# A two-layer encoder step with Strassen products in its channel mixer: loads, copies, additions and splits of the weights put into another order

## The chip, the core and the metric

The kernel runs on one core of one Trainium2 chip, which has a matrix engine (TensorE, PE in the rows), two elementwise engines (VectorE, DVE; ScalarE, ACT), GpSimd (POOL) and SyncE (SP). The metric is the device time in microseconds (us) of one execution. Before the change three runs took 1881.4, 1882.58 and 1882.79 us, so the median is 1882.58 us.

## The reference

Two layers of an encoder, in float32, for a prompt of 528 tokens (16 learned ones and 512) and for 8 running streams of 16 tokens: 656 columns in all, width 1024. Each layer mixes tokens (attention with a latent cache beside a gated recurrence) and then channels. All that the change touches is in the channel mixer:

```python
def conv_ffn(h, p, buf):
    u = h @ p['w_ffn_up']                      # 1024 -> 2 x 2816
    a, v = u[..., :D_FF], u[..., D_FF:]
    ext = jnp.concatenate([buf.astype(a.dtype), a], axis=1)
    c = p['ffn_conv_b'] + sum(ext[:, j:j + T] * w[j] for j in range(3))
    out = (jax.nn.silu(c) * v) @ p['w_ffn_down']   # 2816 -> 1024
    return out, ext[:, -2:]
```

An RMSNorm stands before it and after it, and `x` is added.

## The kernel before, in words

**Layout.** Activations lie with their 1024 features on 128 partitions by 8 tiles, and the 656 tokens along the free dimension, in two halves of 328 (`cols_of(0)`, `cols_of(1)`). Each float32 operand of a product is split into a high part (a copy by ACT into float32r) and a low part (the difference, by DVE), and a product is three matmuls: low weight by high input, high by high, high by low.

**The channel mixer.** The 2816 inner channels are 22 chunks `c` of 128. Chunks 0 to 2 are plain. Chunks 3 to 21 (`NPL` = 3 is the first) are computed with a Strassen scheme, in which the 2x2 blocks are the halves of the 1024 inputs by gate and value weights, and the token halves. A chunk has seven products of 12 matmuls (4 input tiles by 3), in this order: B11, B21, T2, T3, T1, T4, B22. T1 to T4 have sums of weight blocks as weights, and T1 to T3 have sums of input blocks as inputs: `Sf` is such a sum (by DVE, `s_sum`), `Sh` its high and `Sl` its low part (`s_high` by ACT, `s_low` by DVE), slots 0, 1, 2 for T1, T2, T3. T4 and B22 need the second token half of the inputs, of which the lower four tiles of `Hh` and `Hl` are replaced for B22 (`s4_part`).

The chunks form six groups (`GROUPS`): 0-1, 2-5, 6-9, 10-13, 14-17, 18-21. After each group a pass over the down weights (`down_pass`, passes 0 to 5) multiplies its chunks into 8 output tiles `n`. Pass 0 covers the plain chunks 0 and 1 and runs just before chunk 3. In pass 0 ACT copies each tile to `Y`; in later passes DVE adds it to `Y`; in pass 5 DVE and ACT also make the squares for the norm.

**Within a chunk** the PSUM results are taken by `chunk` of ACT (lines 1970 to 1998) and of DVE (2774 to 2802):
- ACT: a convolution step and the `silu` of the chunk before (`pending`), the copy of B11 to `p1` (`act_took` 0), the copy after T2 to `u2` (`act_took` 1), the copy of T3 to `p7` (`act_took` 2), and `g_high` of the chunk before. `p1` and `u2` are halves of `R2` (line 154), whose buffer the rows call R; `p7` is called p.
- DVE: the rest of the convolution (`conv_rest`), two steps that end in `ax`, `times_v` of the chunk before, the low part `g_low` of its result, the addition to `p7` after T1 (`dve_took`), and after T4 the addition to `u2`.
- PE (`chunk`, lines 928 to 975) waits for `act_took` 0 ahead of T2, for `act_took` 1 ahead of T1, for `act_took` 2 ahead of T4, and for `dve_took` ahead of B22. In chunk 3 it also waits for the sums of inputs (`s_split`), which are counted in the order in which DVE makes them.

**Splits of weights.** Weights come in pieces of 512 KB into four raw slots: slots 0 and 1 (`wraw`) and 2 and 3 (`wff`). ACT writes the high part (`w_high`, or `w_high_two` for two half-units that lie side by side), DVE the low part (`w_low`), and DVE's counts `w_split`. A table, `split_after` (lines 502 to 509), says after the end of which PE unit each split may be made; `highs(l, u)` and `lows(l, u)` issue all splits up to unit `u`. With the numbers of this kernel, `highs(l, u0 + B21)` in a later chunk issues the splits of that chunk's own T4 and B22; `highs(l, u0 + T2)` the next chunk's B11 and B21; `highs(l, u0 + T1)` the next T2 and T3; in the pass 0 loop unit `u0` gives chunk 3's T2 and T3, and unit `u0 + 1` its T1 and T4. In chunk 3 `highs(l, u0 + B21)` gives its B22 alone. The last unit of the layer, number `UNITS_L - 1`, is pass 5's last piece and has a buffer of its own (`whi_x`, `wlo_x`).

**What loads.** SP issues the loads of pieces in one fixed order (lines 614 to 654). A load waits until the splits of the piece that was in its slot are done (`earlier`, `last_unit`): the two pieces of chunk c take the slots of chunk c - 2, so that they wait for the splits of that chunk's T4 and B22. SP also loads B22's block into `t2` and `t3`. POOL adds blocks with accumulating DMAs, in one order (lines 781 to 793): for chunk c it issues T1's sum of chunk c + 1 (`sum_t1`, line 736, which waits for that chunk's second piece), then T4's sum of chunk c (`sum_t4`, line 760), then T2's and T3's of chunk c + 1 (lines 744 and 750). In the last chunk of a group T4's sum goes first.

Of the kernel before, what the change touches and what calls it, by code (L numbers as in the profile page):

```python
# [54 lines left out]
P_UP = P_OUT + N_OUT  # L55
# [52 lines left out]
def build(nc, a):  # L108
# [6 lines left out]
    with ctx:  # L115
# [347 lines left out]
        def s_split(l, i):  # L463


            return S_DVE * l + (13, 14, 19, 21)[i]
# [114 lines left out]
        def _(sp):  # L581
# [31 lines left out]

            for g in range(DEPTH * PIECES):
# [29 lines left out]
                if earlier[g] is not None:  # L644
                    sp.wait_ge(S("w_split"), earlier[g] // PIECES * UNITS_L + last_unit(earlier[g] % PIECES) + 1)
                if p == P_CHUNK[NPL]:
                    sp.wait_ge(S("oas_taken"), l + 1)
                    sp.wait_ge(S("ob_split"), HG * (l + 1))
                    sp.wait_ge(S("out"), 32 * (l + 1))
                for s, lo, hi, at in parts_of(p):  # L650
                    sp.dma_start(raw_of(p)[:, at:at + hi - lo], a["wstream"][l, s][:, lo:hi]).then_inc(S(loaded[g][0]), 16)
                for c, p0 in P_CHUNK.items():
                    if p == p0 + 1:
                        sum_parts(l, c)
# [813 lines left out]
        def _(act):  # L1468
# [124 lines left out]
            for l in range(DEPTH):  # L1593
# [376 lines left out]
                def chunk(c, pending):  # L1970
# [10 lines left out]
                    highs(l, u0 - 1)  # L1981
# [6 lines left out]
                    highs(l, u0 + B21)  # L1988
# [11 lines left out]
                for q, (c0, c1) in enumerate(GROUPS):  # L2000
# [11 lines left out]
                    if q == NQ - 1:  # L2012
                        w_high(l, UNITS_L - 1)
                    for n in range(KD):
                        if not q:
                            act.wait_ge(S("down"), down_no(l, q, n))
                            did(f(two(Y[:, n, :]), halves(down_bank(n)), ACT.Copy), "act_took")
                        if not q and n == 5:
                            s_high(Sh[:, 0, :, :], Sf[:, 0, :, :], 18)
                            act.wait_ge(S("tile"), t0 + T_UP + 2 * NPL)  # L2020
                            for x in range(2):
                                s_high(Hh[:, 2 * x:2 * x + 2, cols_of(1)], s4_part(x), 12, -1.0)
                        if q and q < NQ - 1 and nk * (n + 1) % 8 == 0:
                            highs(l, u0 + nk * (n + 1) // 8 - 1)
                        if not q and n >= 5:
                            highs(l, u0 + nk * (n + 1) // 8 - 1)
                exp_table()
                split_to[0] = 0
                for n in range(3):
                    act.wait_ge(S("dve_took"), down_added(l, NQ - 1, n))  # L2030
                    square_x(n0 + N_FFNPOST, n, Y[:, n, :])
                    step(f(Y[:, n, :], Y[:, n, :], ACT.Copy, scale=cols[:, l, C_FFNPOST + n:C_FFNPOST + n + 1]))
                w_high(l + 1, 0)
# [116 lines left out]
        def _(dve):  # L2150
# [173 lines left out]
            for l in range(DEPTH):  # L2324
# [449 lines left out]
                def chunk(c, pending):  # L2774
# [17 lines left out]
                    if pending is not None:  # L2792
                        g_low(pending)
                    after(T1)
                    dve.wait_ge(S("act_took"), act_took(l, c, 2))
                    did(tt_(p7[:, :], p7[:, :], bank(G[s], 0), ALU.add), "dve_took")
                    lows(l, u0 + T1)
# [6 lines left out]
                for q, (c0, c1) in enumerate(GROUPS):  # L2804
# [8 lines left out]
                    else:  # L2813
                        g_low(last_c)
                        lows(l, u0 - 1)
                        for k in range(KH):
                            s_sum(Sf[:, 0, k, :], KH + k, 1, Sf[:, 0, k, :])
                        s_low(2, Sl[:, 0, :, :], Sf[:, 0, :, :], Sh[:, 0, :, :])
                        for x in range(2):
                            s_low(3 + x, Hl[:, 2 * x:2 * x + 2, cols_of(1)], s4_part(x),  # L2820
                                  Hh[:, 2 * x:2 * x + 2, cols_of(1)], -1.0)
# [4 lines left out]
                    if q == NQ - 1:  # L2826
                        w_low(l, UNITS_L - 1)
                    for n in range(KD if q < NQ - 1 else 3):
                        if q:
# [7 lines left out]
                            if q == NQ - 1:  # L2837
                                add_square(n0 + N_FFNPOST, n, n == 0)
                        if q < NQ - 1 and nk * (n + 1) % 8 == 0:
# [220 lines left out]
```

## Time and profile before

| | |
|---|---|
| median of three runs | 1882.58 us |
| the profiled execution | 1880.04 us |
| its span | 1878.2 us |
| granted TensorE clock, mean | 0.992 |
| DVE busy | 1266.8 us, 67% |
| ACT busy | 951.5 us, 51% |
| POOL busy | 230.1 us, 12% |
| HBM read, written | 170.98 MB, 8.65 MB |

The span runs from the first to the last recorded instruction, and 1.84 us of the execution lie outside it. Shares are means over stages with different limits, so the table says who works most and not what a change is worth. The channel mixer's chunks and passes run from about 480 to 925 us in layer 0 and from about 1405 to 1849 us in layer 1.

### The profile page before, as it was taken

Reading aid. Unit: us, or ns where it says so; the run is one execution under the profiler, and the core shown is the slowest. Engines: PE = TensorE matmul, PEld = TensorE weight load, DVE = VectorE, ACT = ScalarE, POOL = GpSimd, SP = SyncE. Lnnn points to the kernel's source line nnn. Section 1 sums busy time; section 2 is a strip of 40 time slices with the busy share of each in tenths; the row PEclk is TensorE's granted clock in tenths of the full one; section 3 lists DMA queues with packets and bytes.
Section 4 is the critical chain, followed back from the end, with each engine's and each line's share of the span. In section 5 each row is a group of like instructions: output and inputs, shape, how many; then the busy total and the mean of one; then the engine's idle time right before and its main releaser. Section 6 shows DMA issues by size and latency. Waiting matters only on the chain.

```text
span 1878.2 us, 31219 instructions
## 1 busy us (share of the span) xinstructions
PE 1803.6 (96%) x11636; PEld 1650.6 (88%) x11636; DVE 1266.8 (67%) x1973; ACT 951.5 (51%) x1593; POOL 230.1 (12%) x257
## 2 busy tenths in 40 slices
PE   8999999999999999999899999999999999999996
PEld 7999976599999999999799999656988999999994
DVE  5777875435775766678767778654377766757777
ACT  6444546435663544535654445564366543635356
POOL 0000023200112121111000000350001121111200
PEclk9999999999999999999999999999999999999998
DMA  5312121411456666655131112314116666666641
GB/s 183 94 58 70 64 74 42 162 45 57 122 140 148 167 152 156 152 152 145 52 108 49 58 65 68 90 48 138 57 50 153 152 147 155 146 162 161 134 106 62
DMA packets 98902, 204.03 MB, mean 109 GB/s; under 512 B 16864, under 2 KB 35680, under 8 KB 98728
## 3 DMA queue, kind: packets, MB, share of 16 engines
q1 hardware_dynamic: 63952, 144.39, 23.8%
q0 software_dynamic: 21888, 39.86, 13.0%
q10 hardware_dynamic: 12912, 17.78, 2.8%
q8 instruction: 94, 1.54, 0.3%
q14 instruction: 56, 0.46, 0.1%
HBM read 170.98 MB, written 8.65 MB: 96 GB/s over the span
## 4 chain that ended last, share of the span: by engine, by line
PE 56%; DVE 17%; ACT 11%; issue 7%; DMA 6%; POOL 1%; ACTq 0%; DVEq 0%; SPq 0%; POOLq 0%
PE G L799 35%; PE WA L799 12%; PE WB L799 7%; DVE wlo L2167 4%; DMA t<-in_wstream 3%; ACT whi L1484 3%; DVE cc L2167 2%; DVE tmp L2167 2%; PE G L803 1%; DMA wraw<-in_wstream 1%; DVE Y L2167 1%; DMA wraw<-t 1%; ACT sq L1484 1%; ACT cc L1484 1%; PE WB L803 1%
## 5 line engine op out<-in xcount | busy, mean ns | idle before, releaser
L799 PE MATMUL G<-Hh,wlo 128*128 128x328 f32 x1384 | 452.3, 327 | 15.5 <-DVE Hl L2167 8.1
L799 PE MATMUL G<-Hh,whi 128*128 128x328 f32 x1384 | 434.4, 314 | 0.0
L799 PE MATMUL G<-Hl,whi 128*128 128x328 f32 x1384 | 433.0, 313 | 0.0
L799 PEld LDWEIGHTS G<-Hh,wlo 128*128 128x128 f32 x1384 | 261.8, 189 | 31.5 <-DVE Hl L2167 12.0
L799 PEld LDWEIGHTS G<-Hh,whi 128*128 128x128 f32 x1384 | 261.9, 189 | 2.3 <-issue 0.4
L799 PEld LDWEIGHTS G<-Hl,whi 128*128 128x128 f32 x1384 | 261.8, 189 | 0.0
L1484 ACT ACTIVATE whi<-wraw 128x1024 fp32r<-128x1024 f32 (+2 forms) x171 | 155.6, 910 | 200.0 <-PE G L799 113.9
L2167 DVE TENSOR_TENSOR wlo<-wraw,whi 128x1024 fp32r<-128x1024 f32 (+2 forms) x171 | 177.5, 1038 | 61.3 <-ACT whi L1484 49.1
L799 PE MATMUL G<-gh,wlo 128*128 128x328 f32 x424 | 134.2, 316 | 9.6 <-DVE tmp L2167 8.8
L799 PE MATMUL G<-gh,whi 128*128 128x328 f32 x424 | 132.8, 313 | 0.0
L799 PE MATMUL G<-gl,whi 128*128 128x328 f32 x424 | 132.1, 312 | 0.0
L799 PE MATMUL G<-Sh,wlo 128*128 128x328 f32 x304 | 98.1, 323 | 13.2 <-ACT R L1484 12.9
L2167 DVE TENSOR_TENSOR wlo<-wff,whi 128x1024 fp32r<-128x1024 f32 (+1 forms) x85 | 86.0, 1012 | 28.1 <-ACT whi L1484 22.1
L1484 ACT ACTIVATE whi<-wff 128x1024 fp32r<-128x1024 f32 (+1 forms) x85 | 75.7, 890 | 48.9 <-PE WB L799 33.0
L799 PE MATMUL G<-Sl,whi 128*128 128x328 f32 x304 | 96.6, 318 | 0.0
L799 PE MATMUL G<-Sh,whi 128*128 128x328 f32 x304 | 96.5, 317 | 0.0
L2167 DVE SCALAR_TENSOR_TENSOR cc<-ax,cols,cc 128x672 f32<-128x672 f32 x88 | 80.8, 919 | 18.4 <-ACT cc L1484 16.2
L799 PEld LDWEIGHTS G<-gh,wlo 128*128 128x128 f32 x424 | 79.7, 188 | 13.5 <-DVE tmp L2167 12.1
L2167 DVE TENSOR_TENSOR Y<-Y,G 128x656 f32<-128x656 f32 (+1 forms) x56 | 42.8, 764 | 55.5 <-PE G L799 52.9
L799 PEld LDWEIGHTS G<-gl,whi 128*128 128x128 f32 x424 | 79.7, 188 | 0.0
L799 PEld LDWEIGHTS G<-gh,whi 128*128 128x128 f32 x424 | 79.7, 188 | 0.0
L1484 ACT ACTIVATE cc<-ax,cols 128x672 f32<-128x672 f32 x44 | 41.8, 951 | 73.3 <-DVE ax L2167 72.2
(327 smaller groups left out, 4098.8 us busy)
## 6 DMA issues: line engine op xcount, KB each, us to landing
wraw<-in_wstream SPq DMA_DIRECT2D x108, 512.0 KB, 3.3
wff<-in_wstream SPq DMA_DIRECT2D x40, 512.0 KB, 4.6
t<-in_wstream SPq DMA_DIRECT2D x76, 256.0 KB, 4.6
t<-in_wstream POOLq DMA_DIRECT2D x38, 256.0 KB, 4.7
ckT<-in_ckT SPq DMA_DIRECT2D x12, 512.0 KB, 3.4
wff<-in_wstream POOLq DMA_DIRECT2D x20, 256.0 KB, 4.3
t<-wff POOLq DMA_DIRECT2D x20, 256.0 KB, 3.3
wff<-t POOLq DMA_DIRECT2D x20, 256.0 KB, 5.6
```

The source lines that it names most:

```text
L799: return pe.matmul(out, lhsT, rhs, start=start, stop=stop, skip_group_check=True)
L803: return pe.transpose(out, in_, ident[0:n, 0:n])
L1484: return act.activation(*args, **kw)
L2167: return kind(*args, **kw)
```

## The change

On SP, the loads of chunk 3's two pieces, and of its `t2` and `t3`, are issued ahead of piece `P_UP + 2` instead of behind pass 0's pieces, and the three waits that guard their memory go with them. On ACT, in pass 0, the copies of `s4_part` into `Hh` come after `Y` tiles 1 and 2, the split of T2 and T3 after tile 3, and the copy into `Sh` slot 0 after tile 5. In chunk 3, and in the second chunk of each later group (7, 11, 15, 19), the split that stood ahead of the `u2` copy comes behind it. On DVE, the low parts of `Hl` and the split of T2 and T3 come ahead of the last sums of inputs, the counts in `s_split` follow, and in every chunk `g_low` comes behind the addition to `p7`. In pass 5 the split of the last unit is moved from ahead of the loop over tiles to behind tile 0's square on ACT, and behind tile 1's on DVE. What PE executes, and its order, is as it was.

```diff
--- before.py
+++ after.py
@@ -463,7 +463,7 @@
         def s_split(l, i):
 
 
-            return S_DVE * l + (13, 14, 19, 21)[i]
+            return S_DVE * l + (13, 14, 21, 16)[i]
 
         S_DVE, S_ACT = 21, KH + 5
 
@@ -610,6 +610,17 @@
                 if j:
                     sp.wait_ge(S("w_split"), unit_of(j - 1, T3) + 1)
                 sp.dma_start(t3[:, :], b22).then_inc(S("t3_in"), 16)
+
+            def piece_in(l, p):
+
+                g = l * PIECES + p
+                if earlier[g] is not None:
+                    sp.wait_ge(S("w_split"), earlier[g] // PIECES * UNITS_L + last_unit(earlier[g] % PIECES) + 1)
+                for s, lo, hi, at in parts_of(p):
+                    sp.dma_start(raw_of(p)[:, at:at + hi - lo], a["wstream"][l, s][:, lo:hi]).then_inc(S(loaded[g][0]), 16)
+                for c, p0 in P_CHUNK.items():
+                    if p == p0 + 1:
+                        sum_parts(l, c)
 
             for g in range(DEPTH * PIECES):
                 if g % PIECES == P_OUT + 5:
@@ -641,17 +652,14 @@
                     sp.wait_ge(S("roped"), 2 * l + 2)
                     turned_rows(1)
                 p = g % PIECES
-                if earlier[g] is not None:
-                    sp.wait_ge(S("w_split"), earlier[g] // PIECES * UNITS_L + last_unit(earlier[g] % PIECES) + 1)
-                if p == P_CHUNK[NPL]:
+                if p == P_UP + 2:
                     sp.wait_ge(S("oas_taken"), l + 1)
                     sp.wait_ge(S("ob_split"), HG * (l + 1))
                     sp.wait_ge(S("out"), 32 * (l + 1))
-                for s, lo, hi, at in parts_of(p):
-                    sp.dma_start(raw_of(p)[:, at:at + hi - lo], a["wstream"][l, s][:, lo:hi]).then_inc(S(loaded[g][0]), 16)
-                for c, p0 in P_CHUNK.items():
-                    if p == p0 + 1:
-                        sum_parts(l, c)
+                    for e in range(P_CHUNK[NPL], P_CHUNK[NPL] + 2):
+                        piece_in(l, e)
+                if p not in (P_CHUNK[NPL], P_CHUNK[NPL] + 1):
+                    piece_in(l, p)
                 if g % PIECES == 6:
                     for i in range(4):
                         sp.dma_start(cos4[32 * i:32 * i + 32, :], a["rope"][64:96, :]).then_inc(S("cos_in"), 16)
@@ -1978,14 +1986,16 @@
                     if pending is not None:
                         conv_first(pending)
                         carry(pending)
-                    highs(l, u0 - 1)
+                    if c != NPL:
+                        highs(l, u0 - 1)
                     after(B11)
                     act.wait_ge(S("ax"), l * KF + c)
                     did(f(p1, bank(G[s], 0), ACT.Copy), "act_took")
                     if pending is not None:
                         silu(pending)
                     halo(c)
-                    highs(l, u0 + B21)
+                    if c not in (NPL, GROUPS[group_of(c)][0] + 1):
+                        highs(l, u0 + B21)
                     after(T2)
                     did(f(u2, bank(G[s], 0), ACT.Copy), "act_took")
                     highs(l, u0 + T2)
@@ -2009,20 +2019,16 @@
                     else:
                         highs(l, u0 - 1)
                     g_high(last_c)
-                    if q == NQ - 1:
-                        w_high(l, UNITS_L - 1)
                     for n in range(KD):
                         if not q:
                             act.wait_ge(S("down"), down_no(l, q, n))
                             did(f(two(Y[:, n, :]), halves(down_bank(n)), ACT.Copy), "act_took")
+                        if not q and n in (1, 2):
+                            act.wait_ge(S("tile"), t0 + T_UP + 2 * NPL)
+                            s_high(Hh[:, 2 * n - 2:2 * n, cols_of(1)], s4_part(n - 1), 12, -1.0)
                         if not q and n == 5:
-                            s_high(Sh[:, 0, :, :], Sf[:, 0, :, :], 18)
-                            act.wait_ge(S("tile"), t0 + T_UP + 2 * NPL)
-                            for x in range(2):
-                                s_high(Hh[:, 2 * x:2 * x + 2, cols_of(1)], s4_part(x), 12, -1.0)
-                        if q and q < NQ - 1 and nk * (n + 1) % 8 == 0:
-                            highs(l, u0 + nk * (n + 1) // 8 - 1)
-                        if not q and n >= 5:
+                            s_high(Sh[:, 0, :, :], Sf[:, 0, :, :], 20)
+                        if q < NQ - 1 and nk * (n + 1) % 8 == 0:
                             highs(l, u0 + nk * (n + 1) // 8 - 1)
                 exp_table()
                 split_to[0] = 0
@@ -2030,6 +2036,8 @@
                     act.wait_ge(S("dve_took"), down_added(l, NQ - 1, n))
                     square_x(n0 + N_FFNPOST, n, Y[:, n, :])
                     step(f(Y[:, n, :], Y[:, n, :], ACT.Copy, scale=cols[:, l, C_FFNPOST + n:C_FFNPOST + n + 1]))
+                    if n == 0:
+                        w_high(l, UNITS_L - 1)
                 w_high(l + 1, 0)
 
                 def scale_y(n, x):
@@ -2789,11 +2797,11 @@
                     if pending is not None:
                         times_v(pending)
                     lows(l, u0 + T2)
-                    if pending is not None:
-                        g_low(pending)
                     after(T1)
                     dve.wait_ge(S("act_took"), act_took(l, c, 2))
                     did(tt_(p7[:, :], p7[:, :], bank(G[s], 0), ALU.add), "dve_took")
+                    if pending is not None:
+                        g_low(pending)
                     lows(l, u0 + T1)
                     after(T4)
                     step(tt_(u2, u2, bank(WA, s), ALU.add))
@@ -2813,18 +2821,17 @@
                     else:
                         g_low(last_c)
                         lows(l, u0 - 1)
+                        for x in range(2):
+                            s_low(2 + x, Hl[:, 2 * x:2 * x + 2, cols_of(1)], s4_part(x),
+                                  Hh[:, 2 * x:2 * x + 2, cols_of(1)], -1.0)
+                        lows(l, u0)
                         for k in range(KH):
                             s_sum(Sf[:, 0, k, :], KH + k, 1, Sf[:, 0, k, :])
-                        s_low(2, Sl[:, 0, :, :], Sf[:, 0, :, :], Sh[:, 0, :, :])
-                        for x in range(2):
-                            s_low(3 + x, Hl[:, 2 * x:2 * x + 2, cols_of(1)], s4_part(x),
-                                  Hh[:, 2 * x:2 * x + 2, cols_of(1)], -1.0)
+                        s_low(4, Sl[:, 0, :, :], Sf[:, 0, :, :], Sh[:, 0, :, :])
                     if q == NQ - 1:
                         did(mark(), "R_used")
                     if q:
                         g_low(last_c)
-                    if q == NQ - 1:
-                        w_low(l, UNITS_L - 1)
                     for n in range(KD if q < NQ - 1 else 3):
                         if q:
                             dve.wait_ge(S("down"), down_no(l, q, n))
@@ -2836,6 +2843,8 @@
                                 step(tt_(y, y, R[:, :], ALU.mult))
                             if q == NQ - 1:
                                 add_square(n0 + N_FFNPOST, n, n == 0)
+                                if n == 1:
+                                    w_low(l, UNITS_L - 1)
                         if q < NQ - 1 and nk * (n + 1) % 8 == 0:
                             lows(l, u0 + nk * (n + 1) // 8 - 1)
                 split_to[0] = 0
```

## Rows read from the trace of the kernel before

**Rows 1.** Part 1 of the page: each engine's busy time, its share, its instructions.

```profile
PE 1803.6 (96%) x11636; PEld 1650.6 (88%) x11636; DVE 1266.8 (67%) x1973; ACT 951.5 (51%) x1593; POOL 230.1 (12%) x257
```

**Rows 2.** Waits of PE, whole span: total us, times, longest us.

```profile
PE G L799 <- ACT R L1484: 12.9, 9, 3.7
...
PE G L799 <- DVE p L2167: 3.7, 14, 0.5
```

**Rows 3.** Timeline of PE, layer 0, chunk 3: start us, us, instruction [idle before].

```profile
521.79 0.31 PE L799 MATMUL G<-Hl,whi 128*128 128x328 f32 x1
525.79 0.61 PE L799 MATMUL G<-Sh,wlo 128*128 128x328 f32 x1 [3.69 <-ACT R L1484]
```

**Rows 4.** Timeline of ACT, end of pass 0 and chunk 3, layer 0.

```profile
517.54 1.30 ACT L1484 ACTIVATE Sh<-Sf 128x1312 fp32r<-128x1312 f32 x1 [1.87 <-DVE Sf L2167]
...
522.12 0.72 ACT L1484 ACTIVATE Y<-G 128x656 f32<-128x656 f32 x1
...
525.25 0.44 ACT L1484 ACTIVATE R<-G 128x328 f32<-128x328 f32 x1
```

**Rows 5.** Timeline of DVE, the same stretch.

```profile
515.16 2.35 DVE L2167 SCALAR_TENSOR_TENSOR Sf<-X,cols,Sf 128x328 f32<-128x328 f32 x4
...
520.51 0.84 DVE L2167 SCALAR_TENSOR_TENSOR Hl<-gh_f,Hh 128x656 fp32r<-128x656 f32 x1
...
522.43 1.23 DVE L2167 TENSOR_TENSOR wlo<-t,whi 128x1024 fp32r<-128x1024 f32 x1
```

**Rows 6.** Timeline of ACT, chunks 15 and 16, layer 0.

```profile
771.64 1.06 ACT L1484 ACTIVATE whi<-wff 128x1024 fp32r<-128x1024 f32 x1
772.79 0.45 ACT L1484 ACTIVATE R<-G 128x328 f32<-128x328 f32 x1
...
785.29 1.38 ACT L1484 ACTIVATE whi<-wraw 128x512 fp32r<-128x512 f32 x2 [1.10 <-DMA wraw<-t]
786.76 0.44 ACT L1484 ACTIVATE R<-G 128x328 f32<-128x328 f32 x1
```

**Rows 7.** Timeline of PE: chunk 15, chunk 16 twice, chunk 20, layer 1's chunk 16.

```profile
772.19 0.32 PE L799 MATMUL G<-Sl,whi 128*128 128x328 f32 x1
...
787.25 0.42 PE L799 MATMUL G<-Sh,wlo 128*128 128x328 f32 x1 [0.30 <-ACT R L1484]
...
791.35 0.42 PE L799 MATMUL G<-Hh,wlo 128*128 128x328 f32 x1 [0.22 <-DVE p L2167]
...
871.92 0.42 PE L799 MATMUL G<-Sh,wlo 128*128 128x328 f32 x1 [1.91 <-ACT R L1484]
...
1713.06 0.46 PE L799 MATMUL G<-Sh,wlo 128*128 128x328 f32 x1 [2.24 <-ACT R L1484]
```

**Rows 8.** Timeline of DVE: chunk 15, chunk 19, layer 0.

```profile
773.08 1.23 DVE L2167 TENSOR_TENSOR wlo<-wff,whi 128x1024 fp32r<-128x1024 f32 x1
...
856.50 1.23 DVE L2167 TENSOR_TENSOR wlo<-wff,whi 128x1024 fp32r<-128x1024 f32 x1
```

**Rows 9.** Timeline of SP and of POOL, chunks 15 and 16, layer 0.

```profile
774.33 0.80 SPq L651 DMA_DIRECT2D wff<-in_wstream  x2
...
779.52 0.87 POOL L736 DMA_DIRECT2D wff<-in_wstream  x1 [7.46 <-DMA wff<-in_wstream]
...
780.06 1.23 POOL L760 DMA_DIRECT2D wraw<-t  x1
```

**Rows 10.** Windows: busy us of PE, PEld, DVE, ACT, POOL (instructions), PEclk, DMA, GB/s.

```profile
871.90:873.70 1.80, 1.78 (x12) 1.79 (x13) 0.78 (x2) 1.50 (x2) 0.00 (x0) 1.00 0.87 138
1713.06:1716.30 3.24, 3.24 (x12) 3.24 (x13) 2.62 (x3) 2.84 (x4) 0.51 (x1) 0.54 0.77 189
```

**Rows 11.** Timeline of DVE, pass 5, layer 0.

```profile
906.22 0.84 DVE L2167 TENSOR_TENSOR acc<-acc,sq 128x656 f32<-128x656 f32 x1 [0.82 <-ACT sq L1484]
907.17 0.84 DVE L2167 TENSOR_TENSOR Y<-Y,G 128x656 f32<-128x656 f32 x1
```

**Rows 12.** Timeline of PE, pass 5, layer 0.

```profile
908.06 0.42 PE L799 MATMUL G<-gh,wlo 128*128 128x328 f32 x1 [0.40 <-DVE Y L2167]
```

## The prediction

> **What bounds the kernel now.** I read the page's busy times first. PE works nearly all the time [rows 1], and the change leaves its work alone, so only PE's idle time can be won or lost. The waits of PE come next [rows 2]. Nine waits end with an ACT copy into R, which is the `p1` or the `u2` copy, and fourteen with DVE's addition to `p7`. I then listed PE's timeline through both layers, to see where each lies. Every matmul of 328 columns follows the last by 0.15 us (twelve in 1.80 us [rows 10]), so a product is due 0.15 us after the last matmul starts, and after a wait the second matmul comes some 0.12 us late again.
>
> Three kinds of wait matter. The first is chunk 3's T2, once in each layer: due at 521.94, it starts at 525.79 [rows 3]. Idle that long, PE comes back at a lower granted clock: twelve matmuls after a wait of 2.24 us take 3.24 us at a granted clock of 0.54 (nearly all of it at the level of 1.2 GHz), not 1.80 at 1.00 (2.4 GHz) [rows 7, 10]. The price is 3.85 + 1.44 = 5.3 us in a layer. The second is T1 of the third chunk of a group (8, 12, 16, 20): all eight start late, from 0.3 us to the 1.91 and 2.24 of [rows 7]. The third is B22 behind `p7` (0.22 us idle [rows 7], some 0.5 in all), nine of them in second and third chunks and most others in a group's last.
>
> **Part 1, chunk 3's loads earlier: 0.** ACT's splits of its pieces find the data there before the change, and SP is otherwise waiting when the four DMAs go out: their place is some 15 us ahead of piece `P_UP + 2`'s own release. What covers them is that nothing else loads there. If they held that piece up it would be by their issue, some 0.4 us each [rows 9], 1.6 us a layer at most.
>
> **Part 2, the order in pass 0: 0.** T2 waits for `p1` at 525.25 [rows 4]. Going back from it on ACT: the split of T1 and T4, `Y` tiles 7 and 6, then T2 and T3's split and the two `Hh` copies, then `Sh` at 517.54, which waits for DVE's `Sf` sums. The change takes the `Hh` copies and T2/T3's split out from behind `Sh`. But DVE now makes two `Hl` parts and T2/T3's low part ahead of these sums. The `Hl` parts take 522.43 - 520.51 = 1.92 us, the low part 1.23 and a gap of 0.03 [rows 5]: 3.18 us. DVE has no idle time there, so the sums start at 518.34 instead of 515.16, and `Sh` at 520.72 instead of 517.54. It ends at 522.02, tile 6 follows at about 522.12, and that is where it is now [rows 4]. Tile 7 and the split of T1 and T4 still come next, since the loop's condition holds at tile 7, and so leaving out `highs(l, u0 - 1)` in chunk 3 leaves out nothing. `p1` stays at 525.25 and the stall stays. In layer 1 ACT does not idle ahead of tile 6, so there I get 0.3 us more. Bounds: -10.6 for both layers if the stall went, +0.6. I take +0.3, as the sums are from durations of the same instructions.
>
> In chunk 3 B22's split moves behind `u2`, some 3 us. The second piece of chunk 5 waits for it on SP, behind it T1's sum of chunk 5 on POOL, and behind that T4's sum of chunk 4, whose split stands ahead of chunk 4's `u2`. That chain has about that much slack: 0 to 0.4 us a layer, and I take 0.3 for both.
>
> **Part 3, splits behind `u2` in chunks 7, 11, 15, 19: a loss.** In chunk 15 ACT splits T4 and B22 at 771.64 and then copies `u2` at 772.79 [rows 6], although T1, which waits for `u2`, was never late in these chunks. Now `u2` goes first. T2's last matmul ends at 772.51 [rows 7], so `u2` runs from 772.54 to 772.99. With a gap of 0.09 as between the two in [rows 6], the split takes 1.06 and ends at 774.16, and DVE's low part starts at 774.20, not 773.08 [rows 8]: 1.12 us late. Who waits for it? SP issues chunk 17's pieces when it ends, at 774.33 [rows 9]. POOL waits for the second of these until 779.52, and only then issues T1's sum, and behind it in its queue T4's sum of chunk 16, at 780.06. That lands ahead of 785.29, where ACT has waited 1.10 us for it [rows 6]; then come the split, `u2` at 786.76, and T1 at 787.25 [rows 7]. Each link is an event that the next waits for, so T1 of chunk 16 starts 1.12 us later still. Where the split is one of 1024 columns this holds for chunks 8, 12 and 16 in both layers: 6 x 1.12 = 6.7 us. In the last group DVE has one more multiplication ahead of the split and reaches it late anyway (856.50 [rows 8]): I take 0.2 for each chunk 20. The clock may add 1.2 us there, as 1.91 us idle left it at 1.00 and 2.24 did not [rows 10]; I leave it to the range. Bounds: 0 (a load that starts later lands as early) to 8 x 1.12 + 2 x 1.4 = 11.8 us.
>
> This can be weighed against a rule. The rows show a load that reaches POOL 5.2 us after its issue [rows 9], while an accumulating DMA of POOL is still under way. In the Trainium skill, page "DMA: Bandwidth & Descriptors", section "Queues, rings and completion order", each DMA engine takes packets in turn from the queues that have work. By that a load issued 1.12 us later shares less with POOL's transfer and lands in less time; if half were made up, this part would be 3.6 us instead of 7.1.
>
> **Part 4, `p7` ahead of `g_low`: a gain.** `g_low` lasts about as long as a wait costs here, and stands between the splits and the addition. With it behind, the addition starts when T1 has ended. Nine waits in second and third chunks, 0.22 idle + 0.16 of overlap + 0.12 at the next matmul, are 0.5 us each: -4.4 us. In a group's last chunk the pass that follows waits for the end of DVE's whole sequence, which is as long as before, so of those I take -0.5 (bounds 0 and -3). `g_low` itself is needed only in the pass.
>
> **Part 5, the last unit moved back: a loss.** Ahead of pass 5's loop both engines waited for PE anyway, so the split cost nothing. Now ACT has it between squares 0 and 1, and DVE between the addition of square 1 and that of `Y` tile 2, for which PE waits. ACT's second square comes 0.6 us later (1.06 of split less its idle time), so DVE adds square 1 at 906.84, not 906.22 [rows 11]. Then come 1.23 us of low part with a gap of 0.09, and tile 2 is added at 909.1, not 907.17. PE has waited for it at 908.06 already [rows 12], so it starts at 910.0: 1.94 us late. The rest of the stage hangs on DVE, with no slack to take it up: 2 x 1.94 = +3.9 us. Bounds: 0 and 4.5.
>
> **Sum.** 0.3 + 0.3 + 6.7 + 0.4 - 4.4 - 0.5 + 3.9 = +6.7 us, that is 1880.04 + 6.7 = 1886.7 us for the profiled execution. This execution is 2.5 us below the median of 1882.58; against the median the sum gives 1889.3, and I say 1889.
>
> **Rivals.**
> - *The first stall goes.* If chunk 3's `p1` no longer stands behind late `Sf` sums (the copies free ACT sooner than I count), 10.6 us go, and the sum is 6.7 - 10.9 = -4.2: 1878.4, faster. For it: the stall is the longest in the mixer, and most moved steps lie around it. Against it: T1 and T4's split and both `Y` tiles still stand ahead of `p1`, and DVE's sums start 3.2 us later. It decides when `Sh` starts at 517.5 instead of 520.7. Chance 0.15.
> - *The third chunks don't get later*, because the loads make up for their later start or T4's sum has slack that I don't see. Then 7.1 us are not lost: 1882.2, no change. For it: the waits ahead of T1 vary from 0.3 to 2.2 us, which speaks for transfers of uneven length. Against it: ACT waited for the DMA in each of them. Chance 0.15.
> - *The last unit is hidden.* Without its 3.9 us, the sum is +2.8: 1885.4, within what counts as no change. Against it: PE waits for that very tile now. Chance 0.1.
> - *The longer stalls take the clock down.* Four or five third chunks with 1.4 us more each: 1895. For it: two stalls are at 2 us already. In the Trainium skill, page "TensorE: Matmul & The Clock Gate", section "HAM oscillation", waits for DMA throttle PE again and again and each time the restart is paid at half the clock. Chance 0.1.
> - The forecast itself, 0.5.
>
> **How the numbers follow.** Some 0.2% (3.8 us) is what a measurement of this kernel can tell from no change, so faster is below 1878.8 and slower above 1886.3. Slower: the forecast, the clock case, less some of the forecast's lower edge: 0.57. No change: the second and third rivals and that edge: 0.27. Faster: the first rival and part of its neighbours: 0.16. The range goes from the first rival, 1878, to 1894, where only the worst of the clock case is left out. The forecast's own range is 1886 to 1892.
>
> **What would show it.** In the changed profile T2 of chunk 3 still waits 3.5 to 4 us on R, with `Sh` 3.2 us later; T1 of chunks 8, 12 and 16 waits a microsecond longer, and POOL's line 736 in the chunk ahead too; the waits on `p7` are nearly gone; and in pass 5 PE waits about 2 us more for `Y`. I am wrong if chunk 3's T2 starts on time, or if POOL's T1 sums come no later after T2 of the second chunk than the 7.0 us of now (772.51 to 779.52 [rows 7, 9]).

## The result, and the profile after

The changed kernel takes 1898.03 us (median of 4 runs, 1897.58 to 1900.73) against 1882.68 us for the kernel before (median of 4, 1881.4 to 1884.51): a ratio of 1.0084, 95% interval 1.0066 to 1.0101, or +15.8 us (+12.4 to +19.0). The direction was predicted, the size was not: 1889 with a range up to 1894. The profiled execution took 1900.73 us, with a span of 1898.9.

Part 1 of the page answers to [rows 1]:

```profile
PE 1814.3 (96%) x11636; PEld 1662.9 (88%) x11636; DVE 1267.5 (67%) x1973; ACT 951.5 (50%) x1593; POOL 230.7 (12%) x257
```

PE has the same 11636 instructions and is busy 10.7 us longer: half of the growth of this execution's span (20.7 us) shows as matmuls at a lower granted clock, not as idle time. (Some 1.6 us of these 20.7 come ahead of the changed code.) The waits of PE, in total us, times, longest us, answer to [rows 2]:

```profile
PE G L807 <- DVE tmp L2175: 13.9, 12, 2.4
PE G L807 <- ACT R L1492: 12.4, 12, 2.3
...
PE G L807 <- issue: 8.4, 4, 4.1
...
PE G L807 <- DVE Y L2175: 5.1, 2, 2.8
```

The row for `p7` (3.7 us, 14 times) is gone, as predicted. The `issue` row holds chunk 3's T2, which stood under R before: without it R was 12.9 - 7.1 = 5.8 us and is now 12.4. And `DVE tmp`, where each pass starts, has grown to 13.9 from this row of the kernel before:

```profile
PE G L799 <- DVE tmp L2167: 8.8, 12, 1.5
```

The ends of the longest waits, from PE's timeline:

```profile
527.79 0.61 PE L807 MATMUL G<-Sh,wlo 128*128 128x328 f32 x1 [4.12 <-issue]
...
794.70 0.42 PE L807 MATMUL G<-Sh,wlo 128*128 128x328 f32 x1 [1.64 <-ACT R L1492]
...
905.67 0.46 PE L807 MATMUL G<-gh,wlo 128*128 128x328 f32 x1 [2.38 <-DVE tmp L2175]
...
919.22 0.41 PE L807 MATMUL G<-gh,wlo 128*128 128x328 f32 x1 [2.75 <-DVE Y L2175]
```

These are chunk 3's T2 (3.69 in [rows 3]), chunk 16's T1 (0.30 in [rows 7]), the start of pass 5, and the wait for `Y` tile 2 (0.40 in [rows 12]). What the clock did behind them and behind layer 1's tile 2, from windows with the columns of [rows 10]:

```profile
527.79:534.22 6.43, 6.42 (x24) 6.43 (x25) 2.51 (x5) 2.50 (x5) 0.00 (x0) 0.53 0.24 84
905.67:910.90 5.23, 5.23 (x24) 5.23 (x25) 0.84 (x1) 2.02 (x2) 0.00 (x0) 0.67 0.01 3
919.20:922.30 3.10, 3.08 (x12) 3.08 (x13) 1.11 (x2) 2.65 (x3) 0.00 (x0) 0.56 0.00 0
1850.00:1855.00 5.00, 4.98 (x23) 4.98 (x24) 3.33 (x6) 4.05 (x7) 0.00 (x0) 0.66 0.00 0
```

At 1.00 (2.4 GHz) twelve such matmuls take 1.80 us; behind tile 2 they take 3.10, so this fall alone is 1.3 us. In layer 0 PE gets it back within the pass: its two later waits there shrink from 0.83 and 1.05 us to nothing and 0.60, and at the pass's end it is 11.2 us late, as ahead of the fall. In layer 1 nothing is given back: 18.0 us late at tile 2, 19.5 at the end of the pass.

Pass 0 and chunk 3 on ACT answer to [rows 4], chunks 15 and 16 to [rows 6]:

```profile
522.74 1.30 ACT L1492 ACTIVATE Sh<-Sf 128x1312 fp32r<-128x1312 f32 x1 [5.44 <-DVE Sf L2175]
...
525.77 1.37 ACT L1492 ACTIVATE whi<-wff 128x512 fp32r<-128x512 f32 x2
527.25 0.44 ACT L1492 ACTIVATE R<-G 128x328 f32<-128x328 f32 x1
...
778.57 0.45 ACT L1492 ACTIVATE R<-G 128x328 f32<-128x328 f32 x1 [1.01 <-PE G L807]
779.12 1.06 ACT L1492 ACTIVATE whi<-wff 128x1024 fp32r<-128x1024 f32 x1
...
792.74 1.37 ACT L1492 ACTIVATE whi<-wraw 128x512 fp32r<-128x512 f32 x2 [1.46 <-DMA wraw<-t]
794.21 0.44 ACT L1492 ACTIVATE R<-G 128x328 f32<-128x328 f32 x1
```

Behind `Sh` ACT now has only `Y` tiles 6 and 7 and the split of T1 and T4 ahead of `p1`, but `Sh` itself starts 5.20 us later by these clocks, of which 1.6 come from the start. In chunk 15 `u2` is now copied ahead of the split. SP and POOL answer to [rows 9], DVE in pass 5 to [rows 11]:

```profile
781.52 0.80 SPq L620 DMA_DIRECT2D wff<-in_wstream  x2
...
786.83 0.87 POOL L744 DMA_DIRECT2D wff<-in_wstream  x1 [9.51 <-DMA wff<-in_wstream]
...
915.69 0.84 DVE L2175 TENSOR_TENSOR acc<-acc,sq 128x656 f32<-128x656 f32 x1 [1.47 <-ACT sq L1492]
917.00 1.23 DVE L2175 TENSOR_TENSOR wlo_x<-wff,whi_x 128x1024 fp32r<-128x1024 f32 x1 [0.47 <-DVE acc L2175]
918.33 0.84 DVE L2175 TENSOR_TENSOR Y<-Y,G 128x656 f32<-128x656 f32 x1
```

Against before, matched matmul by matmul, PE is 3.4 us late after chunk 3 (1.6 of it from the start), 7.3 at the start of layer 0's pass 5, 11.2 behind that pass's tile 2, 14.5 at layer 1's pass 5, 18.0 behind its tile 2. That says where, but not which edit: two parts of the change touch the same chunks. So each part was run alone on the kernel before.

### The profile page after: what moved, and what is told of

Read it like the earlier page. It is cut to its first block, busy times and chain, and to the rows that moved or that the text cites. A ratio compares the mean times of both kernels' runs of the same rounds, so it can differ in the third digit from the quotient of the medians.

```text
span 1898.9 us, 31219 instructions
## 1 busy us (share of the span) xinstructions
PE 1814.3 (96%) x11636; PEld 1662.9 (88%) x11636; DVE 1267.5 (67%) x1973; ACT 951.5 (50%) x1593; POOL 230.7 (12%) x257
## 4 chain that ended last, share of the span: by engine, by line
PE 60%; DVE 18%; ACT 9%; issue 6%; DMA 5%; POOL 1%; DVEq 0%; ACTq 0%; SPq 0%; POOLq 0%
PE G L807 37%; PE WA L807 13%; PE WB L807 8%; DVE wlo L2175 4%; DMA t<-in_wstream 3%; ACT whi L1492 2%; DVE cc L2175 2%; DVE tmp L2175 2%; PE G L811 1%; DMA wraw<-t 1%; ACT cc L1492 1%; DVE Y L2175 1%; ACT sq L1492 1%; DMA wff<-in_wstream 1%; PE WB L811 1%
## 5 line engine op out<-in xcount | busy, mean ns | idle before, releaser
L807 PE MATMUL G<-gh,wlo 128*128 128x328 f32 x424 | 136.2, 321 | 19.1 <-DVE tmp L2175 13.9
L807 PE MATMUL G<-Sh,wlo 128*128 128x328 f32 x304 | 99.2, 326 | 20.7 <-ACT R L1492 12.4
L2175 DVE SCALAR_TENSOR_TENSOR cc<-ax,cols,cc 128x672 f32<-128x672 f32 x88 | 80.9, 919 | 18.4 <-ACT cc L1492 16.2
```

What stands on the lines that cost most here:

```text
L807: return pe.matmul(out, lhsT, rhs, start=start, stop=stop, skip_group_check=True)
L2175: return kind(*args, **kw)
```

## The experiments

A ratio is an estimate from all runs of a kernel against runs of the kernel before on the same chip, with its 95% interval; it can differ from the quotient of the two medians by up to 0.0006. The us beside it are the part above or below 1, times 1882. Absolute times don't compare from chip to chip: the kernel before has a median of 1878.6 us beside the first four experiments, of 1881.63 us beside both changed kernels with a part taken out, the split behind `p1` and the split ahead of `silu`, and of 1881.61 us beside the others.

**The last unit alone.** ACT's `w_high(l, UNITS_L - 1)` goes from ahead of pass 5's loop behind the scaling of `Y` tile 0, DVE's `w_low` behind the addition of square 1:

```
-                    if q == NQ - 1:
-                        w_low(l, UNITS_L - 1)
...
+                                if n == 1:
+                                    w_low(l, UNITS_L - 1)
```

> The kernel before with the last unit's split moved back and nothing else. Theory of the prediction: both engines do 1.06 and 1.23 us of work that was hidden, Y tile 2 comes 1.94 us late in each layer, +3.9 us. Theory from the two traces (the clock counts): the wait for Y tile 2 goes from 0.40 to 2.3-2.7 us idle and the matmuls after it run at a granted clock of about 0.6, some 1.3 us more per layer, less what later waits give back: +5 to +7.5 us. Rival (this part is nothing, the growth is from the other parts): +0 to +1 us.

Measured: 1884.59 us, ratio 1.0029 (1.0018 to 1.0040), +5.5 us (+3.4 to +7.5). PE's wait for tile 2 in the two layers:

```profile
911.03 0.42 PE L799 MATMUL G<-gh,wlo 128*128 128x328 f32 x1 [2.74 <-DVE Y L2167]
...
1836.38 0.42 PE L799 MATMUL G<-gh,wlo 128*128 128x328 f32 x1 [2.39 <-DVE Y L2167]
```

Tile 2 comes 2.3 and 2.0 us later than before, 4.3 us in both layers. In this execution the clock stayed at 1.00 behind 911.03 (window 911.00 to 914.60) and behind 1836.38 (to 1840.00), so the fall seen in the changed kernel doesn't come with every such wait. The interval holds both 3.9 and 7; "nothing" is out.

**The second chunks' splits alone** (part 3).

```
-                    highs(l, u0 + B21)
+                    if c != GROUPS[group_of(c)][0] + 1 or c == NPL:
+                        highs(l, u0 + B21)
```

> The kernel before with the split of T4 and B22 behind the u2 copy in each group's second chunk (7, 11, 15, 19) and nothing else. Theory (the loads that T1's sum of the third chunk waits for are issued a microsecond later, and everything behind them is): +1.12 us in six chunks, a little in the other two, +6 to +7.5 us. Rival (loads that start later share less and land in less time): about +3.5 us. Rival (the chain has slack): 0.

Measured: 1885.4 us, ratio 1.0033 (1.0020 to 1.0046), +6.2 us (+3.8 to +8.7): the size that was predicted. The place is another. DVE's, PE's and POOL's timelines, chunks 15 and 16:

```profile
776.17 1.23 DVE L2168 TENSOR_TENSOR wlo<-wff,whi 128x1024 fp32r<-128x1024 f32 x1 [1.31 <-ACT whi L1484]
...
779.83 0.50 DVE L2168 TENSOR_TENSOR p<-p,G 128x328 f32<-128x328 f32 x1
...
780.38 0.42 PE L799 MATMUL G<-Hh,wlo 128*128 128x328 f32 x1 [0.45 <-DVE p L2168]
...
782.43 0.87 POOL L736 DMA_DIRECT2D wff<-in_wstream  x1 [9.18 <-DMA wff<-in_wstream]
...
790.00 0.42 PE L799 MATMUL G<-Sh,wlo 128*128 128x328 f32 x1 [0.31 <-ACT R L1484]
```

The late low part stands ahead of the addition to `p7` as well, and chunk 15's own B22 waits for that. B22 is 0.7 to 1.0 us late in each of six second chunks (7, 11 and 15 in both layers) (waits on `p7`: 7.5 us in 19, against 3.7 in 14), and T1 of the third chunk then has little left to wait for: 0.31 us here, 0.30 before.

**The addition to `p7` alone** (part 4). `g_low(pending)` goes from ahead of `after(T1)` behind the addition.

> The kernel before with DVE's addition to p7 ahead of g_low and nothing else. Theory of the prediction: nine waits of 0.5 us and a little in the groups' last chunks go, -4.9 us. Theory from the two traces (the wait goes, but T1 of the next chunk or the start of the pass waits 0.3 to 0.5 us longer, and pass 5 starts behind a longer wait with the clock down): -1 to +3 us. They differ in the start of pass 5 too: 1.5 us idle by the first, about 2.2 us and a granted clock of 0.67 behind it by the second.

Measured: 1881.4 us, ratio 1.0018 (1.0006 to 1.0029), +3.4 us (+1.1 to +5.5), where the prediction had -4.9. The group of chunks 10 to 13 in layer 0 shows it. All of PE's waits there, first in the kernel before:

```profile
709.57 0.42 PE L799 MATMUL G<-Hh,wlo 128*128 128x328 f32 x1 [0.23 <-DVE p L2167]
...
722.73 0.42 PE L799 MATMUL G<-Hh,wlo 128*128 128x328 f32 x1 [0.23 <-DVE p L2167]
...
730.78 0.42 PE L799 MATMUL G<-gh,wlo 128*128 128x328 f32 x1 [0.55 <-DVE tmp L2167]
```

and with the addition moved:

```profile
708.44 0.42 PE L799 MATMUL G<-Sh,wlo 128*128 128x328 f32 x1 [0.38 <-ACT R L1484]
...
721.73 0.42 PE L799 MATMUL G<-Sh,wlo 128*128 128x328 f32 x1 [0.19 <-ACT R L1484]
...
733.79 0.42 PE L799 MATMUL G<-gh,wlo 128*128 128x328 f32 x1 [0.94 <-DVE tmp L2167]
```

Both waits on `p7` are gone, and in their place T1 waits for `u2` in chunks 12 and 13, and pass 3 starts 0.39 us more idle. DVE's timeline in chunk 13 gives the reason for the pass. Before (the low part of T1, the addition, the next low part):

```profile
719.78 1.22 DVE L2167 TENSOR_TENSOR wlo<-wraw,whi 128x1024 fp32r<-128x1024 f32 x1 [0.43 <-ACT whi L1484]
...
722.18 0.50 DVE L2167 TENSOR_TENSOR p<-p,G 128x328 f32<-128x328 f32 x1
722.78 1.23 DVE L2167 TENSOR_TENSOR wlo<-wraw,whi 128x1024 fp32r<-128x1024 f32 x1
```

and with the addition moved:

```profile
722.88 1.23 DVE L2167 TENSOR_TENSOR wlo<-wraw,whi 128x1024 fp32r<-128x1024 f32 x1 [0.43 <-ACT whi L1484]
724.24 0.50 DVE L2167 TENSOR_TENSOR p<-p,G 128x328 f32<-128x328 f32 x1
724.84 0.84 DVE L2167 TENSOR_TENSOR gl<-tmp,gh 128x656 fp32r<-128x656 f32 x1
725.79 1.23 DVE L2167 TENSOR_TENSOR wlo<-wraw,whi 128x1024 fp32r<-128x1024 f32 x1
```

From the first low part to B22 it is 2.95 us before and 2.57 now (725.45): PE gains 0.38. From low part to low part it is 3.00 and 2.91, and to the start of the pass 11.00 and 10.91. DVE does the same work in another order, and the start of the pass hangs on it. By ACT's and DVE's rows the two waits of T1 have another source. In chunk 12 the `u2` copy stands behind a split that waits 0.92 us for a DMA (0.91 before). In chunk 13 it goes back, over `silu` and the convolution steps, to another such split (1.11 us for `t`, 0.98 before). Neither comes earlier when PE does. Behind the longer waits the clock fell in two places:

```profile
874.90:878.20 3.30, 3.30 (x15) 3.30 (x14) 2.41 (x3) 2.25 (x3) 0.86 (x1) 0.57 0.94 273
900.95:905.90 4.95, 4.93 (x22) 4.93 (x23) 2.07 (x2) 3.09 (x3) 0.00 (x0) 0.66 0.02 3
1824.20:1829.00 4.80, 4.76 (x31) 4.76 (x32) 2.90 (x3) 3.10 (x3) 0.00 (x0) 1.00 0.00 0
```

The second window is the start of layer 0's pass 5, whose wait rose from 1.48 to 1.98 us: 22 matmuls where before 4.95 us (898.40 to 903.35) hold 33. Layer 1's start (2.12 us, third window) kept its clock. So more than the idle time is paid.

Rows of one execution need care here. The 12.9 us on R in [rows 2] hold the 2.24 us of layer 1's chunk 16 [rows 7]. In the profiles of the last unit, of pass 0 and of the loads alone, which leave this place as it was, that wait isn't there, and T1 of the eight third chunks waits 2.2 to 2.4 us in all, against 5.9 in the profile before and 4.5 with part 4. Matched against the profile of the loads alone, both mixers together: with part 4 B22 comes 8.5 us earlier, the starts of the passes take back 4.2, T1 of the third chunks 2.4, the other T1 and T2 2.5, and the clock and what else is left 3.0. That sums to +3.6 us, as measured.

**Pass 0's order alone** (part 2, with chunk 3's B22 split behind `u2`).

> The kernel before with the new order of splits, sums and copies in pass 0, and B22's split of chunk 3 behind u2; the loads and all else as before. Theory of the prediction: chunk 3's T2 waits as before, 0 in layer 0 and 0.3 us in layer 1, +0.3 to +0.6 us. Theory from the two traces: T2 waits 0.4 us longer in both layers and in one of them the slow clock lasts over T3 too, +1 to +2 us. Rival (the copies free ACT and the stall goes): -10 us.

Measured: 1879.95 us, ratio 1.0001 (0.9993 to 1.0010), +0.2 us. T2 waits 4.10 and 3.75 us (3.69 and 3.40 before): the stall stays, and what is added can't be told from nothing.

**Chunk 3's loads alone** (part 1).

> The kernel before with chunk 3's weights loaded four pieces ahead and nothing else. Theory of the prediction: nothing waits for these loads and nothing else loads there: 0, at most +1.6 us a layer by their issue. Rival (the parts measured alone sum to less than the changed kernel without the p7 part, +15.6 us against 11.9, so the missing part sits here): +3 to +4 us, with ACT or DVE later in the stretch ahead of chunk 3.

Measured: 1882.22 us, ratio 1.0005 (0.9994 to 1.0016), +0.9 us: nothing that can be told. The five parts alone sum to 5.5 + 6.2 + 3.4 + 0.2 + 0.9 = 16.2 us, the whole change is 15.8. How they add up is the next question.

**The changed kernel without the last unit's move.**

> The changed kernel with the last unit's split put back to its old place, ahead of pass 5's loop. The last unit alone cost 5.5 us on the kernel before. If the parts add up, this kernel is 5 to 6 us faster than the changed one, +9 to +11 us against before (ratio about 1.0052). If the parts share a cost (pass 5 starts at a low clock here, so that the wait for Y tile 2 costs less or more), it differs from that by 1.5 us or more.

Measured: 1892.54 us, ratio 1.0058 (1.0046 to 1.0071), +10.9 us, 4.9 less than the whole. The last unit adds up with the rest, as far as intervals of some 4 us on such a difference can tell.

**The changed kernel with the old order of `p7` and `g_low`.**

> The changed kernel with DVE's addition to p7 behind g_low as before. Alone this part cost 3.4 us. If the parts add up: 3 to 4 us faster than the changed kernel, +11 to +13 us against before. Rival: with the split of T4 and B22 behind u2, DVE's low part is late in each second chunk, and then p7 ahead of g_low saves more than alone, because the addition behind both is on B22's path (0.8 us idle in six second chunks in the trace of that part alone): the changed kernel would be as fast as this one or faster, +15 to +18 us.

Measured: 1896.66 us, ratio 1.0083 (1.0069 to 1.0097), +15.6 us: in the changed kernel part 4 is worth 0.2 us, with an interval of some 4 us to either side. The -4.9 of the prediction is outside it; the +3.4 that part 4 costs alone is not.

**Parts 3 and 4 together on the kernel before.**

> The kernel before with two parts: T4's and B22's split behind u2 in each group's second chunk, and the addition to p7 ahead of g_low. Alone they cost 6.2 and 3.4 us. If they add up: +9 to +10 us. If the second hides the first's wait at B22 (0.46 to 0.81 us idle in six second chunks) and that comes back at T1 of the third chunk: +6 to +7 us, with no wait on p7 in the second chunks and T1 of chunks 8, 12, 16 waiting 1.2 to 1.4 us.

Measured: 1889.69 us, ratio 1.0042 (1.0026 to 1.0057), +7.9 us (+4.9 to +10.7). It lies between the two expectations, and the interval holds both. The trace shows what the rival said: no wait on `p7`, and the third chunks' T1 waits longer, as here in chunk 16 (0.31 with part 3 alone):

```profile
792.34 0.42 PE L799 MATMUL G<-Sh,wlo 128*128 128x328 f32 x1 [1.70 <-ACT R L1484]
```

**`g_low` cut short.** If part 4 gained nothing because DVE's sequence kept its length, a shorter sequence should gain. This kernel leaves out most of `g_low`'s work, so `gl` holds old values:

```
-                        g_low(pending)
+                        g_low(pending, 82 if pending >= 6 else T)
```

> The kernel before with g_low cut from 656 columns to 82 in all but the last chunks of groups 2 to 5 (24 instructions; the rest of gl keeps an older chunk's values), in its old place. The addition to p7 is then on time as in the changed kernel, but DVE's sequence gets 0.7 us shorter instead of keeping its length. If the moved addition gained nothing because g_low had filled DVE's wait for T1 and then held up the rest of DVE's chunk, here the gain stays: -4 us or more (7 or more waits of 0.5 us per pair of layers, and shorter waits at the start of the passes). If the next wait of PE hangs on ACT's splits and their DMAs and takes back whatever PE gains: 0 to -2 us.

Measured: 1876.31 us, ratio 0.9972 (0.9962 to 0.9983), -5.3 us (-7.2 to -3.2). PE's waits in this kernel, and below them those with part 4 alone:

```profile
PE G L799 <- ACT R L1484: 13.3, 13, 3.7
...
PE G L799 <- DVE tmp L2167: 9.0, 12, 1.5
```

```profile
PE G L799 <- DVE tmp L2167: 13.5, 12, 2.1
PE G L799 <- ACT R L1484: 12.5, 13, 3.7
```

Neither has a row for `p7`. With the sequence shorter the passes start as early as before (9.0 us; 8.8 before), with it only reordered they take back 4.7 us. The waits on R, which hang on ACT's splits and their DMAs, take back their part in both, and this kernel's clock also fell once behind such a wait (chunk 20, 2.54 us). Matched against the profile of the loads alone as above, B22 gains the same 8.5 us as with part 4, but the starts of the passes take back nothing (-0.3) where part 4 lost 4.2; T1 of the third chunks takes 3.2.

**The stall of chunk 3, taken on directly.** In the kernel before, chunk 3's split of T1 and T4 stands behind the `p1` copy, on DVE behind the additions to `p1`:

```
-                        if not q and n >= 5:
+                        if not q and n in (5, 6):
                             highs(l, u0 + nk * (n + 1) // 8 - 1)
...
-                    highs(l, u0 - 1)
+                    if c != NPL:
+                        highs(l, u0 - 1)
```

> The kernel before with one thing else: in chunk 3 the split of T1 and T4 (1.5 us on ACT) stands behind the p1 copy, not ahead of it. My reading of the chain ahead of chunk 3's T2 is that Sh, the split, two Y tiles and that split follow each other without a gap, so p1 is copied 1.5 us earlier: T2's idle falls from 3.7 to 2.2 us, -3 us for both layers, and -1 to -3 us more if the clock doesn't fall behind the shorter wait. Rival: DVE or T1 becomes late instead by the same amount, 0.

Measured: 1880.4 us, ratio 0.9993 (0.9981 to 1.0005), -1.3 us, not told from nothing. T2's idle falls by 1.5 us in each layer, to 2.19 and 1.91 us, just as the chain said. But in layer 1 chunk 4's T2 then waits 1.10 us for its own `p1`, where it had not waited before: most of that layer's gain is taken back fourteen us later.

**The opposite of part 3.** In chunks 7, 11, 15 and 19 the split goes ahead of `silu` and its low part ahead of `times_v`.

> The kernel before with the opposite of the change's second-chunk part: in chunks 7, 11, 15 and 19 T4's and B22's split goes ahead of silu on ACT and its low part ahead of times_v on DVE, about a microsecond earlier. Theory (loads of the third chunk wait for it, and T1 of the third chunk for them): T1 of chunks 8, 12, 16 comes up to 1.1 us earlier where it waits (0.3 to 2.2 us idle now), -3 to -6 us with the clock. Rival (times_v and silu come late and B22 or T1 of the same chunk waits): 0 to +5 us.

Measured: 1880.4 us, ratio 0.9993 (0.9984 to 1.0003), -1.3 us, not told from nothing. T1 of layer 0's chunk 20 no longer waits (1.91 us before, 1.3 us and more in every profile that leaves it alone), but those of chunks 12 and 16 wait 0.43 and 0.51 us, no less than before: there the earlier split gained nothing.

**Both orders together.**

> The kernel before with the two other orders together: chunk 3's split of T1 and T4 behind the p1 copy, and T4's and B22's split ahead of silu in each group's second chunk. Each alone measured a ratio of 0.9993. If both gains are real and add up: about -2.5 us, faster than both kernels by just over what can be told. If they were noise: 0.

Measured: 1877.06 us, ratio 0.9975 (0.9965 to 0.9985), -4.7 us (-6.6 to -2.8). It beats both kernels. The two alone sum to -2.6, and the intervals don't tell that from -4.7. Its waits of PE, where R had 12.9 us in [rows 2]:

```profile
PE G L799 <- DVE tmp L2170: 9.1, 12, 1.5
...
PE G L799 <- ACT R L1484: 8.7, 9, 2.2
...
PE G L799 <- DVE p L2170: 5.0, 20, 0.5
```

In this profile the clock did not fall behind chunk 3's T2 in either layer, where it fell in both layers before. With only the split behind `p1` it fell in layer 0. The windows behind T2 in layer 0, first of both orders together (2.21 us idle), then of the split behind `p1` alone (2.19 us idle):

```profile
524.99:530.00 5.01, 3.53 (x23) 3.56 (x24) 3.91 (x6) 4.23 (x9) 0.86 (x1) 1.00 0.17 52
524.85:530.00 5.15, 3.66 (x16) 3.69 (x17) 3.94 (x6) 3.96 (x9) 0.86 (x1) 0.74 0.24 56
```

## Why the prediction was wrong

By its own sum, beside what each part measures alone:

| Part | predicted | measured |
|---|---|---|
| 1, loads | 0 | +0.9 (-1.1 to +3.0) |
| 2, pass 0 | +0.6 | +0.2 (-1.3 to +1.9) |
| 3, splits behind `u2` | +7.1 | +6.2 (+3.8 to +8.7) |
| 4, `p7` ahead of `g_low` | -4.9 | +3.4 (+1.1 to +5.5) |
| 5, last unit | +3.9 | +5.5 (+3.4 to +7.5) |
| sum | +6.7 | +16.2; the change +15.8 |

**The step that failed is part 4**: "Nine waits in second and third chunks ... are 0.5 us each: -4.4 us". Alone it is 8.3 of the 9.5 us by which the sums differ. (Nine times 0.5 is 4.5 and not 4.4, a slip without weight.) Parts 3 and 4 together were put at +2.2 us and measure +7.9 (+4.9 to +10.7). The waits went, with the size that was said (0.5 us each in second and third chunks, matched against before). But the step priced a wait by its own length and did not ask what PE waits for next. For a group's last chunk the prediction did ask: "the pass that follows waits for the end of DVE's whole sequence, which is as long as before". There the whole gain comes back and more: -0.5 was put down, and the starts of the passes take 4.2 us, which the shorter `g_low` shows to be DVE's sequence. In the chunks ahead PE next waits for a `u2` copy behind ACT's splits and their DMAs, and T1 takes back a part with the shorter `g_low` too. `g_low` filled no idle time of DVE either: in chunk 13 T1's last matmul starts at 720.38 and ends by 720.7, ahead of the end of the low part at 721.00. The clock, put at nothing in this part, is the rest. The profile of the whole change, matched against that of the loads alone, shows the same: B22 comes 8.6 us earlier, but T1 of the third chunks takes 9.2, the starts of the passes 4.9, the other T1 and T2 3.6, chunk 3's T2 1.2, pass 5 behind its start 6.8 and the rest 2.3, which sums to 19.3 us in this execution.

**Part 3** had the right total, and alone it had it by luck, by a chain that was only half of it. "Who waits for it?" named SP, POOL and the next chunk, and missed the addition to `p7` behind the same low part on DVE, in the same chunk. With part 3 alone the loss stands there; in the changed kernel part 4 hides it, and the loss stands where it was predicted, at T1 of the third chunk (+1.34 us in chunk 16). So the two parts are not a loss and a gain that can be added.

The rule of the Trainium skill's page "DMA: Bandwidth & Descriptors", section "Queues, rings and completion order" (each DMA engine takes packets in turn from the queues that have work) was weighed as making half of the later issue good; the half is the prediction's own estimate. From issue to POOL's sum it is 5.19 us in chunk 15 before (774.33 to 779.52), 5.01 with part 3 alone and 5.31 in the changed kernel (781.52 to 786.83): nothing was made good there. In chunk 7 it is 5.67 before and 5.02 and 4.96 after, which looks like 0.7 us made good. But the kernels that issue this load as before show that it is not: with the last unit alone it takes 5.11 (613.31 to 618.42), with pass 0 alone 5.02 and with the loads alone 5.08, so the 5.67 belongs to one execution. Over the eight second chunks the mean is 5.2 us with part 3 alone and 5.3 to 5.4 in those three: 0.1 to 0.2 of the 1.12 us were made good, not half.

**Part 5** was right in its mechanism: DVE waits 1.47 us for ACT's square instead of 0.82, then come the low part and tile 2. Alone the wait grows by 2.3 and 2.0 us instead of 1.94; in the rows of the changed kernel DVE has a gap of 0.47 us ahead of the low part where I took 0.09. Of the +5.5 us these waits are 4.3, and the interval reaches down to 3.4; in the changed kernel the clock fell behind both waits as well.

**Parts 1 and 2** were right. `Sh` came 5.2 - 1.6 = 3.6 us late (3.2 predicted), T2 0.4 us.

**The signs that were named** all came: T2 of chunk 3 waits 4.12 and 3.78 us (3.5 to 4 were named), POOL's T1 sum for chunk 16 comes 8.3 us after T2 of chunk 15 (7.0 before), T1 of the third chunks is late, the waits on `p7` are gone, and PE waits 2 us more for `Y`. None of them looked at what PE waits for once `p7` is out of the way, so they could not show the error.

**The rivals.** The first stall stayed. The third chunks got later. The last unit was not hidden. "The longer stalls take the clock down", with 1895 us, came nearest, though not at its place: it was to strike third chunks, and struck the start of pass 5 and tile 2, and chunk 3's T3. It was given 0.1 and counted on top of a sum that had part 4 as a gain. The Trainium skill's section "HAM oscillation" on the page "TensorE: Matmul & The Clock Gate" says that waits for DMA bring the clock down again and again. The waits for tile 2 are for DVE and ACT, and the traces agree for them in part: behind the wait for tile 2 it fell to 0.56 in the changed kernel, and stayed at 1.00 in the run of that part alone.

What is left open: how much of each part is clock. It differs between executions of one kernel by as much as a part is worth, and one profile of each can't tell.

## What to carry to other kernels

When a wait of the busiest engine is removed, follow the released time to its next wait, and ask whether the engine that it hung on has less to do up to there, or the same in another order; only the first is a gain. A step moved back is late for everything behind it on its engine: list all of that, in the same chunk too, and not only the longest chain. Look at a wait in more than one profile before you price it: the 2.24 us ahead of T1, on which the prediction's price of a low clock leaned, belong to one execution. And measure parts of a change on the kernel before as well as taken out of the changed one, since one part can hide where another's loss stands.

## What the runs showed of the hardware

Between 1.9 and 2.8 us the length of a wait does not say whether the clock falls behind it. After 1.91 us idle the granted clock was 1.00 in the kernel before [rows 10]; behind the same wait of chunk 20, 1.90 us long, it went down to 0.57 with part 4 alone (window 874.90 to 878.20). At the start of pass 5 it was 0.66 behind 1.98 us and 1.00 behind 2.12 us in the same execution (part 4 alone). Behind `Y` tile 2 it was 0.56 after 2.75 us in the changed kernel and 1.00 after 2.74 us with the last unit alone. Each such fall cost PE 1.3 to 1.5 us where it came, and once, behind tile 2 in layer 0 of the changed kernel, shorter waits gave all of it back within the pass.

Waits that hang on DMAs differ between executions by more than these edits move: T1 of layer 1's chunk 16 waited 2.24 us in the profile before and not at all in the three profiles that leave it alone.
